# Moving the weights of the first unit and the order of the logits pairs in a fused encoder layer

## The chip, the cores and the metric

The kernel runs on one core of one Trainium2 chip. The metric is the device time of one execution in microseconds. The kernel before took 1164.75 us in the median of three runs (1164.25 to 1165.76). TensorE is called PE in the profile, VectorE DVE, ScalarE ACT, GpSimd POOL, SyncE SP.

## The reference

One layer of a streaming encoder over 640 tokens (512 of a prompt, 8 streams of 16 new frames), all in float32:

```python
def trunk_layer(x, pos, k_past, v_past, idxk_past, conv_prev, ...):
    x = x + 0.5 * swiglu(rmsnorm(x, ffn1_norm), ffn1_w_gate, ffn1_w_up, ffn1_w_down)
    h = rmsnorm(x, mix_norm)
    z = h @ w_in
    gb, gc, xv, q, k, v, qi, ki, wi = jnp.split(z, SPLIT_POINTS, axis=-1)
    conv_out = gb * conv                       # conv: 3 taps over gc * xv
    ...
    attn = dsa_attention(q, qi, wi, k_all, v_all, ki_all, pos, n_sel)
    x = x + jnp.concatenate([conv_out, attn], axis=-1) @ w_out
    x = x + 0.5 * swiglu(rmsnorm(x, ffn2_norm), ffn2_w_gate, ffn2_w_up, ffn2_w_down)
    return x, k, v, ki, conv_state
```

The width is 1024, the feed-forward parts have 2816 hidden columns. dsa_attention scores every key with a small indexer, keeps the best keys of each query (top_k), and does a masked softmax over them with 8 heads that share 2 key/value heads.

## The kernel before

Activations lie transposed, 128 of the 1024 columns to a chunk `c` (8 chunks), with 640 tokens along the free axis. A product of float32 accuracy is three products of rounded halves: of each operand there is a high half (`xh`, `wh`, written by ACT as a rounded copy) and a low half (`xl`, `wl`, which DVE writes as the difference), and PE multiplies high by high, low by high and high by low. Weights come in units of 128 x 2048 into `raw[:, slot]`, two slots in turn; a unit is split into halves (`split_hi`/`split_lo`, in quarters with `quarter_hi_of`/`quarter_lo_of`) once PE has used the unit two before it.

The program is: a feed-forward part `ffn(0)`, the projection of tokens with the indexer, the attention with the conv and output projections, and `ffn(1)`. Every engine has its own program, written out by hand in one order, and semaphores join them. Nothing is scheduled by a planner, but tables of numbers (`parts_by`, `issued_by`, `QUARTERS`, `ROUNDS`, `CONV_SPLITS`) say in which item a piece is put, on all engines at once.

**The first unit.** `first_unit` (L630 to L646) multiplies chunk by chunk as weights and activations arrive. Its weights are loaded in five pieces (`load_part`, L356), each with the chunk's gate columns and its up columns, 1024 columns apart in `raw`. Ahead of it PE does 16 float32 products of a tile of ones (`WARM_UP`, L988).

**A feed-forward part.** Four plain units come first. `plain_hid(3)` (L1647 and L1651) is what is left of the fourth: two DVE operations over 640 columns. It stands before the last pair of sets, `period(PAIRS - 1, ...)`. ACT's `rest_hi` later reads what it wrote.

**The attention.** There are 40 items, `ITEMS`: five token tiles in the order 3, 4, 2, 1, 0, of 8 heads or streams each. Tile 4 holds the streams' new frames (items 8 to 15, `logits_sample`, one to an item); the other tiles have `logits_pair` (L937), which puts the logits of items n and n+1 (n even) into banks 4 and 5. A pair needs both banks free, so it waits until DVE has read the logits of the two items before. What follows the logits of an item n:

- DVE: `masked_min(n)` (L2115; L2109 in tile 4) copies the masked logits out, finds their minimum and frees the bank;
- ACT: `exp_out(n)` (L1418; L1414 in tile 4);
- DVE, ACT or POOL: `normalise(n)`; from item 12 on it is POOL (L2353, L2354);
- PE: `turn_weights(n)` (L854) transposes the weights, ACT copies them out (`weights_out`), and PE multiplies them with the values: `weigh_sample_values(n)` (L965) in tile 4, else `weigh_four_heads(n)` (L979) in each fourth item.

In one pass of the loop over n, PE turns item n, issues the logits up to `issued_by(n)`, then does the parts up to `parts_by(n)` (`filler`: 6 matmuls of the conv or output projection, L596, L598, L600), then weighs. Items 12, 20, 28 and 36 have no part (`WITHOUT_PART`), and item 8 has none either, by `parts_by`. Four (after item 7) or eight (before) parts are a job, whose result DVE adds up in `proj_out`: L2077 for the output projection. On DVE the same loop has, in this order: `attended_lo` of a finished tile (L2134), `conv_lo`, `masked_min` of the items issued, top-8 rounds (`top_rounds`, L2062 and L2063, by the table `ROUNDS`) of the tiles still to come, `proj_out`, and the low half of a quarter of weights (`quarter_lo_of`, L1557).

Of the kernel before, what the change touches and what calls it, by code (L numbers as in the profile page):

```python
# [27 lines left out]
P = 128  # L28
# [44 lines left out]
def trunk(nc, xt, gu1, dn1, gu2, dn2, wtok, wconv, wout, small, gains, kcache, vcache, ikcache,  # L73
          conv_past, tables, bf_tables, x_keep, y_out, k_out, v_out, ik_out, conv_out):
    with ExitStack() as ctx:
# [154 lines left out]
        proj_job = sem("proj_job")  # L230
        proj_evac = sem("proj_evac")
# [69 lines left out]
        def parts_by(n):  # L301

            if n < 8:
                return 4 * (n + 1)
            return 32 + n - 8 - sum(m <= n for m in WITHOUT_PART)
# [11 lines left out]
        PROJ_SPLITS = {0: U_CONV + 5, item_of(9): U_OUT}  # L317
        QUARTERS = {14 + q: (U_OUT + 1, q) for q in range(4)}
# [4 lines left out]
        def issued_by(n):  # L323

            return min(n + 3 if n < 15 else 19 if n == 15 else n + 5, len(ITEMS))
# [4 lines left out]
        CONV_SPLITS = {8: (0,), 9: (1,), 10: (2,), 11: (3,)}  # L330
# [14 lines left out]
        def chunk_cols(flat, i):  # L345

            a, b = W_CHUNKS[i]
            return flat.rearrange("p (m n) -> p m n", m=2)[:, :, P * a:P * b]

        def quarters_before(U):  # L350
            return 3 * (0 if U == U_CONV else U - U_OUT)
# [232 lines left out]
        def _(pe):  # L584
# [41 lines left out]
            def first_unit():  # L626
# [3 lines left out]
                for c in range(C):  # L630
# [3 lines left out]
                    for m in range(2):  # L634
                        for o, t in zip(outs[m], cols):
                            pe.matmul(o, weight(wh, 0, 8 * m + c), xh[:, c, t], start=(c == 0), stop=False)
                    pe.wait_ge(*((part_lo, i + 1) if i < 4 else (lo_ready, 1)))
                    for m in range(2):
                        for o, t in zip(outs[m], cols):
                            pe.matmul(o, weight(wl, 0, 8 * m + c), xh[:, c, t], start=False, stop=False)  # L640
                    pe.wait_ge(xl_ready, c + 1)
                    for m in range(2):
                        for o, t in zip(outs[m], cols):
                            mm = pe.matmul(o, weight(wh, 0, 8 * m + c), xl[:, c, t], start=False,
# [245 lines left out]
            def proj_part(b, c):  # L890

                U = U_CONV + b // 2 if b < NPROJ else U_OUT + (b - NPROJ) // 4
                if c == 0:
                    pe.wait_ge(lo_ready, U + 1)
                    if U in (U_CONV, U_OUT + 1, U_OUT + 2):
# [204 lines left out]
        def _(act):  # L1100
# [34 lines left out]
            def ffn(k):  # L1135
# [212 lines left out]

                for n in (1, 2):
# [157 lines left out]
            for n in range(len(ITEMS)):  # L1507
                if n == 8 * (n // 8) in (8, 16):
                    attended_hi(n // 8 - 1)
                if n in CONV_SPLITS:  # L1510
                    act.wait_ge(proj_job, NPROJ)
# [10 lines left out]
                if n in QUARTERS and ITEMS[n][0] != 4:  # L1522
# [3 lines left out]
                if n in QUARTERS and ITEMS[n][0] == 4:  # L1526
# [9 lines left out]
        def _(dve):  # L1536
# [62 lines left out]
            def ffn(k):  # L1599
# [342 lines left out]
                plain_hid(3)  # L1942
# [301 lines left out]
            for n in range(len(ITEMS)):  # L2244
# [6 lines left out]
                for ahead in range(issued_by(n - 1), issued_by(n)):  # L2251
                    masked_min(ahead)
# [12 lines left out]
                if n in (25, 33):  # L2265
                    attended_lo(n // 8 - 1)
# [210 lines left out]
```

## Time and profile before

| | us |
|---|---|
| three runs | 1164.25, 1164.75, 1165.76 |
| the profiled execution | 1166.49 |
| its span, first to last instruction | 1164.6 |
| PE busy | 1154.6 |
| DVE busy | 916.1 |
| ACT busy | 526.1 |
| POOL busy | 94.7 |

The mean granted clock of TensorE is 0.994 of full speed. The profile comes from one execution. Busy shares are those of the whole span; a line's instructions are found by the line number. The numbers behind "idle before" in a timeline say how long an engine had stood still before the instruction, and what released it.

### The profile page before, as it was taken

Reading aid. Unit: us, or ns where it says so; the run is one execution under the profiler, and the core shown is the slowest. Engines: PE = TensorE matmul, PEld = TensorE weight load, DVE = VectorE, ACT = ScalarE, POOL = GpSimd, SP = SyncE. Lnnn points to the kernel's source line nnn. Section 1 sums busy time; section 2 is a strip of 40 time slices with the busy share of each in tenths; the row PEclk is TensorE's granted clock in tenths of the full one; section 3 lists DMA queues with packets and bytes.
Section 4 is the critical chain, followed back from the end, with each engine's and each line's share of the span. In section 5 each row is a group of like instructions: output and inputs, shape, how many; then the busy total and the mean of one; then the engine's idle time right before and its main releaser. Section 6 shows DMA issues by size and latency. Waiting matters only on the chain.

```text
span 1164.6 us, 20299 instructions
## 1 busy us (share of the span) xinstructions
PE 1154.6 (99%) x7704; PEld 1107.3 (95%) x7704; DVE 916.1 (79%) x1402; ACT 526.1 (45%) x791; POOL 94.7 (8%) x130
## 2 busy tenths in 40 slices
PE   9999999999999999999999899999999999999999
PEld 9999999999999999867987679999999999999998
DVE  6998777877989982467998753798877778798996
ACT  6354444444445552361234452434444444454452
POOL 0000000000000000102473351000000000000000
PEclk9999999999999999999999899999999999999999
DMA  7212221222332233201321023321322222124222
GB/s 249 85 55 91 86 95 72 98 82 67 124 146 80 73 109 119 73 37 37 145 73 37 1 67 107 129 73 37 109 72 84 96 72 98 64 100 154 103 87 84
DMA packets 22992, 103.98 MB, mean 89 GB/s; under 512 B 3344, under 2 KB 6288, under 8 KB 13584
## 3 DMA queue, kind: packets, MB, share of 16 engines
q1 hardware_dynamic: 21792, 99.67, 24.2%
q10 hardware_dynamic: 1136, 3.43, 1.0%
q8 instruction: 43, 0.70, 0.3%
q14 instruction: 21, 0.17, 0.0%
HBM read 96.99 MB, written 6.10 MB: 89 GB/s over the span
## 4 chain that ended last, share of the span: by engine, by line
PE 91%; DVE 7%; issue 1%; ACT 1%; DVEq 0%; POOL 0%; ACTq 0%; POOLq 0%
PE ps L656 18%; PE ps L658 18%; PE ps L657 18%; PE ps L596 8%; PE ps L600 8%; PE ps L598 8%; PE ps L587 2%; PE ps L589 2%; PE ps L588 2%; DVE score L2063 1%; PE ps L854 1%; DVE top L2062 1%; DVE wl L1548 1%; PE ps L937 1%; PE ps L863 1%
## 5 line engine op out<-in xcount | busy, mean ns | idle before, releaser
L1102 ACT ACTIVATE wh<-raw 128x1024 fp32r<-128x1024 f32 (+4 forms) x206 | 202.4, 985 | 261.6 <-PE ps L658 142.9
L656 PE MATMUL ps<-xs,wh 128*128 128x320 f32 x976 | 300.2, 308 | 0.5 <-ACT snap L1102 0.5
L657 PE MATMUL ps<-xs,wh 128*128 128x320 f32 x976 | 300.2, 308 | 0.0
L658 PE MATMUL ps<-xs,wl 128*128 128x320 f32 x976 | 300.1, 308 | 0.0
L656 PEld LDWEIGHTS ps<-xs,wh 128*128 128x128 f32 x976 | 182.9, 187 | 1.0 <-issue 1.0
L658 PEld LDWEIGHTS ps<-xs,wl 128*128 128x128 f32 x976 | 182.9, 187 | 0.0
L657 PEld LDWEIGHTS ps<-xs,wh 128*128 128x128 f32 x976 | 182.9, 187 | 0.0
L596 PE MATMUL ps<-xh,wh 128*128 128x320 f32 x544 | 131.1, 322 | 0.0
L1672 DVE TENSOR_TENSOR wl<-raw,wh 128x1024 fp32r<-128x1024 f32 (+1 forms) x108 | 112.7, 1044 | 19.4 <-ACT wh L1102 18.3
L600 PE MATMUL ps<-xh,wl 128*128 128x320 f32 x544 | 124.7, 311 | 0.0
L598 PE MATMUL ps<-xl,wh 128*128 128x320 f32 x544 | 124.6, 311 | 0.0
L1102 ACT ACTIVATE snap<-ps 128x320 f32<-128x320 f32 x156 | 68.0, 437 | 121.1 <-PE ps L658 120.6
L596 PEld LDWEIGHTS ps<-xh,wh 128*128 128x128 f32 x544 | 90.0, 189 | 12.6 <-issue 11.1
L598 PEld LDWEIGHTS ps<-xl,wh 128*128 128x128 f32 x544 | 91.8, 189 | 0.0
L600 PEld LDWEIGHTS ps<-xh,wl 128*128 128x128 f32 x544 | 91.7, 189 | 0.0
L658 PE MATMUL ps<-xr,wl 128*128 128x320 f32 x288 | 88.9, 309 | 0.0
L656 PE MATMUL ps<-xr,wh 128*128 128x320 f32 x288 | 88.9, 309 | 0.0
L657 PE MATMUL ps<-xr,wh 128*128 128x320 f32 x288 | 88.9, 309 | 0.0
L1672 DVE TENSOR_TENSOR wl<-sums,wh 128x1024 fp32r<-128x1024 f32 x36 | 44.1, 1225 | 38.1 <-ACT wh L1102 38.1
L1102 ACT ACTIVATE wh<-sums 128x1024 fp32r<-128x1024 f32 x52 | 54.8, 1053 | 24.0 <-DVE sums L1687 14.4
L1548 DVE TENSOR_TENSOR wl<-raw,wh 128x2048 fp32r<-128x2048 f32 (+2 forms) x31 | 56.5, 1823 | 11.5 <-ACT wh L1102 11.5
L1783 DVE TENSOR_TENSOR wl<-raw,wh 128x1024 fp32r<-128x1024 f32 (+1 forms) x48 | 49.9, 1041 | 6.1 <-ACT wh L1102 6.1
(282 smaller groups left out, 2134.4 us busy)
## 6 DMA issues: line engine op xcount, KB each, us to landing
raw<-gu SPq DMA_DIRECT2D x42, 1024.0 KB, 4.8
raw<-dn SPq DMA_DIRECT2D x16, 1024.0 KB, 5.3
raw<-dn SPq DMA_DIRECT2D x12, 512.0 KB, 3.8
raw<-wconv SPq DMA_DIRECT2D x6, 1024.0 KB, 4.9
raw<-wout SPq DMA_DIRECT2D x4, 1024.0 KB, 4.8
x<-xt SPq DMA_DIRECT2D x12, 320.0 KB, 4.7
raw<-wtok SPq DMA_DIRECT2D x4, 840.0 KB, 4.3
x_keep<-x SPq DMA_DIRECT2D x8, 320.0 KB, 2.2
```

The costliest lines, as they stand in the source:

```text
L587: pe.matmul(out, ah, bh, start=first, stop=False)
L588: pe.matmul(out, ah, bl, start=False, stop=False)
L596: pe.matmul(o, ah, bh[:, c], start=first, stop=False)
L598: pe.matmul(o, ah, bl[:, c], start=False, stop=False)
L600: last_mm = pe.matmul(o, al, bh[:, c], start=False, stop=last)
L656: pe.matmul(out, ah, bh, start=first, stop=False, skip_group_check=True)
L657: pe.matmul(out, ah, bl, start=False, stop=False, skip_group_check=True)
L658: return pe.matmul(out, al, bh, start=False, stop=last, skip_group_check=True)
L1102: return nc.scalar.activation(out, in_, ACT.Copy, scale=scale)
L1548: dve.tensor_tensor(wl[:, slot, 0:n], raw[:, slot, 0:n], wh[:, slot, 0:n].bitcast(F32), ALU.subtract).then_inc(lo_ready, 1)
L1672: dve.tensor_tensor(ring(wl_flat, part), set_source(slot, part), ring(wh_flat, part).bitcast(F32), ALU.subtract)\
L1783: dve.tensor_tensor(ring(wl_flat, part), set_source(slot, part), ring(wh_flat, part).bitcast(F32), ALU.subtract)\
```

## The change

Four things change.

1. The first unit of `ffn(0)` lies chunk by chunk in memory, and so in `raw`, `wh` and `wl`: the gate and up columns of one chunk side by side. PE reads weight tile 2c+m in place of 8m+c.
2. `plain_hid(3)` is issued by DVE inside the last period of a feed-forward part (the one with `ahead=False`), in place of before the last two; ACT waits for `hid_ready` before `rest_hi(1)`.
3. Item 8 gets a part, so that from there on each item does the part that was the next one's. With that go: `conv_hi`/`conv_lo` one item earlier (7 to 10), now released by a count of PE's part 27, `chunks_used`; and the weights of unit `U_OUT` split in quarters in items 4 to 7, in place of whole in item 3.
4. From item 15 on, PE issues logits behind the parts, and DVE does `masked_min` last in an item. `issued_by` is n+4 there and not n+5, so that pairs fall into odd items (15, 17, 19, ...) and not into even ones (15 for the first, then 16, 18, ...). ACT splits the quarter of item 15 before that item's `exp_out`.

```diff
@@ parts_by
-            return 32 + n - 8 - sum(m <= n for m in WITHOUT_PART)
+            return 32 + n - 7 - sum(m <= n for m in WITHOUT_PART)
...
-        PROJ_SPLITS = {0: U_CONV + 5, item_of(9): U_OUT}
-        QUARTERS = {14 + q: (U_OUT + 1, q) for q in range(4)}
+        PROJ_SPLITS = {0: U_CONV + 5}
+        QUARTERS = {4 + q: (U_OUT, q) for q in range(4)}
+        QUARTERS |= {14 + q: (U_OUT + 1, q) for q in range(4)}
...
-            return min(n + 3 if n < 15 else 19 if n == 15 else n + 5, len(ITEMS))
+            return min(n + 3 if n < 15 else n + 4, len(ITEMS))
...
-        CONV_SPLITS = {8: (0,), 9: (1,), 10: (2,), 11: (3,)}
+        CONV_SPLITS = {7: (0,), 8: (1,), 9: (2,), 10: (3,)}
@@ chunk_cols
-            return flat.rearrange("p (m n) -> p m n", m=2)[:, :, P * a:P * b]
+            return flat[:, 2 * P * a:2 * P * b]
@@ first_unit, three places
-                            pe.matmul(o, weight(wh, 0, 8 * m + c), xh[:, c, t], start=(c == 0), stop=False)
+                            pe.matmul(o, weight(wh, 0, 2 * c + m), xh[:, c, t], start=(c == 0), stop=False)
@@ proj_part
+                if b == NPROJ - 1 and c == 3:
+                    mm.then_inc(chunks_used, 1)
@@ PE, the loop over the items
-                for ahead in range(issued_by(n - 1), issued_by(n)):
-                    logits(ahead)
+                if n < 15:
+                    for ahead in range(issued_by(n - 1), issued_by(n)):
+                        logits(ahead)
                 for i in range(parts_by(n - 1), parts_by(n)):
                     filler(i)
+                if n >= 15:
+                    for ahead in range(issued_by(n - 1), issued_by(n)):
+                        logits(ahead)
@@ ACT, ffn and the items
+                act.wait_ge(hid_ready, PLAIN * (k + 1))
                 for n in (1, 2):
                     rest_hi(n)
...
-                    act.wait_ge(proj_job, NPROJ)
+                    act.wait_ge(chunks_used, 1)
...
-                if n in QUARTERS and ITEMS[n][0] != 4:
+                if n in QUARTERS and (ITEMS[n][0] != 4 or n == 15):
@@ DVE, period
+                    if not ahead:
+                        plain_hid(3)
                     out_of(p, slot, 0, block)
...
-                plain_hid(3)
                 period(PAIRS - 1, 0, pair_block(PAIRS - 1))
@@ DVE, the items
-                for ahead in range(issued_by(n - 1), issued_by(n)):
-                    masked_min(ahead)
+                if n < 15:
+                    for ahead in range(issued_by(n - 1), issued_by(n)):
+                        masked_min(ahead)
...
+                if n >= 15:
+                    for ahead in range(issued_by(n - 1), issued_by(n)):
+                        masked_min(ahead)
@@ the layout on the host, gate_up
+        if first_by_chunk:
+            plain[0] = plain[0].reshape(P, 2, C, P).transpose(0, 2, 1, 3).reshape(P, 2 * C * P)
```

What it does to the order of PE in item 15. Before, from the turn of item 15 on (`tab` holds the identity, L854 is the turn, L937 the pair, L596 to L600 a part, L965 the weighing):

```order
L854 MATMUL ps<-tab,score 128x128 [waits bank6_free,p_sample_ready]
L854 MATMUL ps<-tab,score 128x128 x2
L937 MATMUL ps<-kt,q_all 128x384 [waits bank5_free,bank4_free]
L937 MATMUL ps<-kt,q_all 128x384
L596 MATMUL ps<-xh,wh 128x320 x2
L598 MATMUL ps<-xl,wh 128x320 x2
L600 MATMUL ps<-xh,wl 128x320 x2
L965 MATMUL ps<-hid,ikc_v 64x64 [waits bank6_free]
L965 MATMUL ps<-hid,ikc_v 64x64
L965 MATMUL ps<-hid,zkv 64x64
L965 MATMUL ps<-hid,ikc_v 64x64 x2
L965 MATMUL ps<-hid,zkv 64x64
```

After, from the same turn on (L856 is the turn, L598 to L602 a part, L941 the pair):

```order
L856 MATMUL ps<-tab,score 128x128 [waits bank6_free,p_sample_ready]
L856 MATMUL ps<-tab,score 128x128 x2
L598 MATMUL ps<-xh,wh 128x320 x2
L600 MATMUL ps<-xl,wh 128x320 x2
L602 MATMUL ps<-xh,wl 128x320 x2
L941 MATMUL ps<-kt,q_all 128x384 [waits bank5_free,bank4_free]
L941 MATMUL ps<-kt,q_all 128x384
L969 MATMUL ps<-hid,ikc_v 64x64 [waits bank6_free]
L969 MATMUL ps<-hid,ikc_v 64x64
L969 MATMUL ps<-hid,zkv 64x64
L969 MATMUL ps<-hid,ikc_v 64x64 x2
L969 MATMUL ps<-hid,zkv 64x64
```

The part, which stood behind the pair (18, 19), now stands ahead of it; the pair comes last before the weighing. The next pair, (20, 21), stood behind the turn of item 16 and now stands behind the part of item 17.

What it does to the order of DVE from `masked_min(16)` in item 14 on. Before (L2115 is `masked_min`, L2062 and L2063 a top-8 round, L1557 a quarter):

```order
L2115 ISA rp,stat<-ps,mask 128x384 [waits bank6_full,mask_ready,bank4_full]
L2115 ISA stat 128x1
L2062 MAX top8<-score 128x8
L2063 MATCH_REPLACE score<-top8,score 128x256 [waits vector_chain]
L1557 TENSOR_TENSOR wl<-raw,wh 128x512 [waits quarter_hi,vector_chain]
L2115 ISA rp,stat<-ps,mask 128x384 [waits bank6_full,mask_ready,bank5_full]
L2115 ISA stat 128x1
L2115 ISA hid,stat<-ps,mask 128x384 [waits bank6_full,mask_ready,bank4_full]
L2115 ISA stat 128x1
L2062 MAX top8<-score 128x8
L2063 MATCH_REPLACE score<-top8,score 128x256 [waits vector_chain]
```

After (L2125, L2072 and L2073, L1566):

```order
L2125 ISA rp,stat<-ps,mask 128x384 [waits mask_ready,bank6_full,bank4_full,vector_chain]
L2125 ISA stat 128x1
L2072 MAX top8<-score 128x8
L2073 MATCH_REPLACE score<-top8,score 128x256 [waits vector_chain]
L1566 TENSOR_TENSOR wl<-raw,wh 128x512 [waits quarter_hi,vector_chain]
L2072 MAX top8<-score 128x8
L2073 MATCH_REPLACE score<-top8,score 128x256 [waits vector_chain]
L1566 TENSOR_TENSOR wl<-raw,wh 128x512 [waits quarter_hi,vector_chain]
L2125 ISA rp,stat<-ps,mask 128x384 [waits bank6_full,mask_ready,bank5_full]
L2125 ISA stat 128x1
L2125 ISA hid,stat<-ps,mask 128x384 [waits bank6_full,mask_ready,bank4_full]
L2125 ISA stat 128x1
```

`masked_min(17)`, which frees bank 5 for the pair (18, 19), stood behind the round and the quarter of item 14. It has moved behind those of item 15 as well. The `attended_lo` of item 16 (L2134, then L2144) keeps its place between `masked_min(18)` and `masked_min(19)`.

## Rows read from the trace of the kernel before

**Rows 1.** The page, part 1: engine, busy us, share of the span, instructions.

```profile
PE 1154.6 (99%) x7704; PEld 1107.3 (95%) x7704; DVE 916.1 (79%) x1402; ACT 526.1 (45%) x791; POOL 94.7 (8%) x130
```

**Rows 2.** Waits of PE, whole span: reader, releaser, us in total, times, longest.

```profile
PE ps L937 <- DVE stat L2115: 4.0, 3, 2.4
...
PE ps L656 <- ACT snap L1102: 0.5, 2, 0.2
```

**Rows 3.** Stretches of 2 us: length, busy us by engine, PEclk, DMA.

```profile
658.00:660.00 2.00, 0.09 (x2) 0.12 (x2) 1.25 (x4) 1.07 (x3) 1.59 (x2) 0.81 0.00 0
...
672.00:674.00 2.00, 2.00 (x11) 1.08 (x10) 1.89 (x4) 0.86 (x3) 1.45 (x2) 0.78 0.00 0
```

**Rows 4.** Timeline of PE: start, length, instruction, idle before it.

```profile
637.96 0.47 PE L965 MATMUL ps<-hid,ikc_v 128*64 128x64 f32 x6 [0.35 <-ACT hid L1102]
...
638.93 0.55 PE L854 MATMUL ps<-tab,rp 128*128 128x128 f32 x3 [0.26 <-DVE rp L2127]
...
640.37 0.56 PE L596 MATMUL ps<-xh,wh 128*128 128x320 f32 x2
...
641.45 0.50 PE L965 MATMUL ps<-hid,ikc_v 128*64 128x64 f32 x6
...
656.97 0.55 PE L854 MATMUL ps<-tab,score 128*128 128x128 f32 x3
659.91 1.65 PE L937 MATMUL ps<-kt,q_all 64*128 64x384 f32 x4 [2.39 <-DVE stat L2115]
...
663.38 0.75 PE L965 MATMUL ps<-hid,ikc_v 128*64 128x64 f32 x6
...
664.49 0.90 PE L854 MATMUL ps<-tab,rp 128*128 128x128 f32 x3
666.53 1.65 PE L937 MATMUL ps<-kt,q_all 64*128 64x384 f32 x4 [1.14 <-DVE stat L2115]
668.12 0.90 PE L596 MATMUL ps<-xh,wh 128*128 128x320 f32 x2
...
669.88 0.84 PE L854 MATMUL ps<-tab,rp 128*128 128x128 f32 x3
```

**Rows 5.** Timeline of DVE in the same place.

```profile
650.26 0.56 DVE L2109 TENSOR_REDUCE stat<-ps 128x1 f32<-128x384 f32 x1 [0.56 <-PE ps L926]
...
655.93 0.82 DVE L2077 SCALAR_TENSOR_TENSOR x<-ps,x 128x640 f32<-128x640 f32 x1
656.67 0.55 DVE L2115 CUSTOM_DVE_ANT_0 rp<-ps,mask 128x384 f32<-128x384 f32 x1
...
657.14 0.42 DVE L2062 MAX8 top<-score 128x8 f32<-128x256 f32 x1
...
658.59 0.69 DVE L1557 TENSOR_TENSOR wl<-raw,wh 128x512 fp32r<-128x512 f32 x1 [0.51 <-ACT wh L1102]
659.20 0.55 DVE L2115 CUSTOM_DVE_ANT_0 rp<-ps,mask 128x384 f32<-128x384 f32 x1
...
661.56 0.56 DVE L2115 CUSTOM_DVE_ANT_0 hid<-ps,mask 128x384 f32<-128x384 f32 x1 [1.80 <-PE ps L937]
...
665.23 0.69 DVE L2134 TENSOR_TENSOR xl<-ps,xh 128x512 fp32r<-128x512 f32 x1 [1.04 <-ACT xh L1102]
```

**Rows 6.** Timeline of POOL: the scaling of one item's weights.

```profile
661.23 0.59 POOL L2354 TENSOR_SCALAR rp<-rp,stat 128x384 f32<-128x384 f32 x1
```

**Rows 7.** Timeline of DVE in the first feed-forward part.

```profile
266.85 0.83 DVE L1651 TENSOR_TENSOR hid<-hid,glu_u 128x640 f32<-128x640 f32 x1
...
279.93 0.49 DVE L1706 TENSOR_TENSOR quart<-ps,snap 128x320 f32<-128x320 f32 x1 [0.87 <-PE ps L658]
```

**Rows 8.** Timeline of all engines at the start.

```profile
1.18 6.74 PE L988 MATMUL ps<-ones 128*128 128x128 f32 x32 [1.18 <-POOL cstate L2302]
...
6.83 0.42 DVE L1606 TENSOR_TENSOR wl<-raw,wh 128x256 fp32r<-128x256 f32 x1 [6.83 <-ACT wh L1102]
...
7.68 0.82 PE L636 MATMUL ps<-xh,wh 128*128 128x320 f32 x4
```

More of the change, by code:

```diff
@@ L230, in trunk @@
         proj_job = sem("proj_job")
+        chunks_used = sem("chunks_used")
         proj_evac = sem("proj_evac")
@@ L347, in chunk_cols @@
             a, b = W_CHUNKS[i]
-            return flat.rearrange("p (m n) -> p m n", m=2)[:, :, P * a:P * b]
+            return flat[:, 2 * P * a:2 * P * b]
         def quarters_before(U):
-            return 3 * (0 if U == U_CONV else U - U_OUT)
+            return 3 * (0 if U == U_CONV else 1 + U - U_OUT)
         def first_part(buf, i):
@@ L639, in first_unit @@
                         for o, t in zip(outs[m], cols):
-                            pe.matmul(o, weight(wl, 0, 8 * m + c), xh[:, c, t], start=False, stop=False)
+                            pe.matmul(o, weight(wl, 0, 2 * c + m), xh[:, c, t], start=False, stop=False)
                     pe.wait_ge(xl_ready, c + 1)
@@ L643, in first_unit @@
                         for o, t in zip(outs[m], cols):
-                            mm = pe.matmul(o, weight(wh, 0, 8 * m + c), xl[:, c, t], start=False,
+                            mm = pe.matmul(o, weight(wh, 0, 2 * c + m), xl[:, c, t], start=False,
                                            stop=(c == C - 1))
@@ L894, in proj_part @@
                     pe.wait_ge(lo_ready, U + 1)
-                    if U in (U_CONV, U_OUT + 1, U_OUT + 2):
+                    if U in (U_CONV, U_OUT, U_OUT + 1, U_OUT + 2):
                         pe.wait_ge(quarter_lo, quarters_before(U) + 3)
@@ L1525, in _ @@
                     exp_out(ahead)
-                if n in QUARTERS and ITEMS[n][0] == 4:
+                if n in QUARTERS and ITEMS[n][0] == 4 and n != 15:
                     quarter_hi_of(*QUARTERS[n])
@@ L2399, in lay_out, with gate_up @@
     x_all = np.concatenate([a["x_prompt"].reshape(SEQ, D), a["x_sample"].reshape(NB * NT, D)])
-    def gate_up(g, u):
+    def gate_up(g, u, first_by_chunk):
         both = np.stack([g[0], u[0]]).reshape(2, C, P, NF, P)
         plain = both[:, :, :, :PLAIN].transpose(3, 2, 0, 1, 4).reshape(PLAIN, P, 2 * C * P)
+        if first_by_chunk:
+            plain[0] = plain[0].reshape(P, 2, C, P).transpose(0, 2, 1, 3).reshape(P, 2 * C * P)
         sets = both[:, :, :, PLAIN:].reshape(2, C, P, PAIRS, 2, P)
@@ L2430, in lay_out @@
         "xt": x_all.reshape(TOK, C, P).transpose(2, 1, 0),
-        "gu1": gate_up(a["ffn1_w_gate"], a["ffn1_w_up"]), "dn1": down(a["ffn1_w_down"]),
-        "gu2": gate_up(a["ffn2_w_gate"], a["ffn2_w_up"]), "dn2": down(a["ffn2_w_down"]),
+        "gu1": gate_up(a["ffn1_w_gate"], a["ffn1_w_up"], True), "dn1": down(a["ffn1_w_down"]),
+        "gu2": gate_up(a["ffn2_w_gate"], a["ffn2_w_up"], False), "dn2": down(a["ffn2_w_down"]),
         "wtok": np.stack([filled(cols(tok[h * 512:(h + 1) * 512, s:s + n]))
```

## The prediction

> **What bounds the kernel now.** I read the page first: PE is busy for 1154.6 of 1164.6 us [rows 1], so no more than 10 us can come from waits, unless matmuls themselves run slow somewhere. Then the waits of PE: most of what the trace explains is one line, the logits pair, which waits 4.0 us in three places for DVE's `masked_min`; a set of a feed-forward part waits 0.5 us in two places [rows 2]. Then the stretches of 2 us: the granted clock is full everywhere but for one place. In 658 to 660 it is 0.81, so 0.76 us of these 2 us ran at half speed (0.19 / 0.5 x 2) and the clock fell at 659.24; in 672 to 674 it is 0.78, so it rose at 672.88 [rows 3]. For 13.64 us PE ran at 1.2 GHz and not at 2.4 GHz. The timeline of PE shows what went ahead: the pair (18, 19) of item 15 waits 2.39 us for `masked_min(17)`, and the clock falls 1.72 us into this wait; the pair (20, 21) waits 1.14 us, and the clock rises 6.35 us after that wait ends [rows 4]. Of the 13.64 us, PE stood still for 0.67 us (659.24 to 659.91) and for 1.14 us. The other 11.83 us would have taken half as long, so the low clock costs 5.9 us: more than all waits of the place together. The change works in this place.
>
> **The start.** The first unit's chunks now come as one run per partition and not as two. PE's warm-up takes from 1.18 to about 7.7 us; the low half that the first unit needs is begun by DVE at 6.83 and takes 0.42 us, and the first real matmul runs at 7.68 [rows 8]. The data is there 0.4 us before PE is. A load that comes sooner is hidden by the warm-up, and copies and matmuls keep their shapes: 0. Were the warm-up no cover, it would be worth 0.4 us at most.
>
> **The move of `plain_hid(3)`.** Its two operations stand before the next-to-last period, and 266.85 is the second of them [rows 7]; the work behind it comes late, and PE waits for a snapshot. That wait occurs once in each feed-forward part, 0.5 us in all [rows 2]. In the last period DVE has nothing to prepare for a next set; it stood still for 0.87 us before its first output, at 279.93 [rows 7]. Two operations of 0.83 us there push this output by about 0.8 us, and the wait for PE's next products behind it absorbs that. Saved 0.5 us (bounds: 0 if the wait moves along, 0.5). ACT's new wait costs nothing: what stands ahead of it waits for the end of the last set, and that set needs an output which DVE gives behind `plain_hid(3)`. Queued behind the wait are `rest_hi` 1 and 2.
>
> **A part in item 8.** A part and what surrounds it take 1.08 us (640.37 to 641.45 [rows 4]). PE's two small waits, 0.35 us in item 8 and 0.26 us in item 9 [rows 4], go, since ACT's copy and DVE's scaling keep their time while PE comes later. So every item from 9 to 15 starts 1.08 - 0.61 = 0.47 us later with one part more done: 0.61 us saved. The splits moved with it (conv, quarters of `U_OUT`) fall in items where each engine keeps up; a quarter is 0.69 us of DVE and replaces, four for one, a split of the whole unit. I take 0, with 0.5 us lost as the other bound.
>
> **The pair (18, 19).** From `masked_min(14)` at 650.26 on, DVE has no gap except for one of 0.51 us for ACT, until `masked_min(17)` at 659.20 [rows 5]: DVE itself sets the wait. That is 8.94 us. Out of it goes `proj_out(12)` (655.93 to 656.67: 0.74), which now belongs to item 11. Into it come a top-8 round (0.94: it starts at 657.14 and its three instructions fill DVE until 658.08) and the quarter of item 15 (0.61, 658.59 to 659.20). So 9.75 us. `masked_min(14)` comes with PE's item 12, at 650.73, `masked_min(17)` at 660.48, and the pair 0.71 us behind it as before: 661.19. PE is done with turn 15 at 657.52 + 0.47 and with the part, half of 1.76 us (668.12 to 669.88 at the low clock [rows 4]), at 658.87. The wait is 2.32 us. It stays: what the part fills, the later `masked_min` opens again. Saved 0.07 us.
>
> **The clock.** With a wait of the same length, work ahead of it of about the same kind, I take it that the clock falls as before, 1.72 us into the wait, at 660.6, and rises 6.35 us after the last long wait. If that is now this one, it rises at 667.5. Then 6.35 us of work run at the low clock and cost 3.2 us, where it was 5.9: 2.7 us saved. This is the largest term, and it hangs on the second wait.
>
> **The pair (20, 21).** It now stands in item 17 behind the part. At the low clock PE needs from 661.19: the pair 1.65, the weighing 1.11, turn 0.90, part 1.76, turn 0.84 [rows 4]: 667.45, then a part at full clock 0.88: 668.33. DVE: `masked_min(18)` 1.65 behind the pair; `attended_lo` 1.85 us behind the start of the weighing (663.38 to 665.23 [rows 4, 5]), at 664.69, 0.61 long; a round, 666.24; `proj_out(13)` only when PE's part of item 16 is done (661.19 + 1.65 + 1.11 + 0.90 + 1.76 = 666.61), until 667.44; a quarter, 668.05; `masked_min(19)` and the 0.71 us: 668.76. So this wait is 0.43 in place of 1.14 us: 0.71 saved. Behind it, by the same durations, the pair (22, 23) waits some 0.2 us for `masked_min(21)`, which is new.
>
> **The sum.** 0.5 + 0.61 + 0.07 + 2.7 + 0.71 - 0.2 = 4.4 us. The profiled execution took 1166.49 us and becomes 1162.1; it lies 1.74 us above the median, so against the median of 1164.75 the forecast is 1160.4 us.
>
> On the price of the clock the Trainium skill (TensorE: Matmul & The Clock Gate, Terms) counts the throttled time times (1 - K/N), idle or not. By that the stretch of before costs half of 13.64, 6.8 us, and that of after half of 6.9, 3.5 us: the gain would be 3.4 and the forecast 1159.7 us. The trace shows PE idle in 1.8 us of it, which no clock can shorten [rows 3, 4], and the sum stays with that.
>
> **Rivals.**
> - The clock never falls. For it: one more part of dense matmuls lies just before the wait. Against it: the wait has its old length. PE then comes to the pair (20, 21) at about 665.2, but DVE, bound by the exponential of item 18 and its own queue, frees bank 5 only for 667.5. The gain is 1.3 us more than forecast, 5.7 us: 1159.1 us.
> - The clock survives the first wait and falls in the second, which is then 2.3 us long. 5.7 - 3.2 = 2.5 us gained: 1162.3 us.
> - The low clock lasts as long as before, since a pair, a weighing and a turn follow the wait again, and between 659.91 and 665.39 such work did not raise it. Then 5.9 us are lost as before, and 4.4 - 2.7 = 1.7 us are gained: 1163.1 us.
> - Slower: pairs come too late for their turns. From the start of `masked_min` to the end of POOL's scaling pass 2.62 us (659.20 to 661.82 [rows 5, 6]), 4.0 with the pair and the first of two ahead of it, and the odd item's `masked_min` stands behind one more round. PE has turns 18 and 19, two parts, a pair and the weighing between, some 4.9 us at full clock. If ACT and POOL are a microsecond late, each item waits, and the clock stays down to about item 24 (685): 24 us of low clock cost 12.0, not 3.2 us, and 4.4 becomes -4.4: 1169.2 us. It turns slower once low-clock work exceeds 6.35 + 2 x 4.4 = 15 us. Against it: at the low clock PE leaves more room, not less.
>
> **Chances.** Forecast 0.50, never falls 0.08, falls in the second wait 0.14, as long as before 0.18, slower 0.10. A measurement of this kernel tells 0.2%, 2.3 us, from no change. The forecast (its own range 1159.2 to 1162), the first rival and most of the second are faster by more than that, and a little of the third: 0.72. The rest of these two is within it: 0.18. The slower case has 0.10. The range from 1158.6 to 1164.6 us leaves out that case and a little at the lower end.
>
> **What would show it.** PE's waits: none at items 8 and 9, none for the snapshot at about 271 us, one of about 2.3 us for the pair (18, 19), one below 0.6 for (20, 21). The granted clock: one stretch below full speed, about 7 us long. The start: the first real matmul at 7.7 us as before. Wrong would be a first wait below 1.5 us, a stretch at the low clock over 10 us, or waits of turns for POOL behind item 18.

## The result

| | us (median) | lowest to highest | executions |
|---|---|---|---|
| before | 1164.75 | 1163.61 to 1166.27 | 9 |
| after | 1168.45 | 1168.05 to 1170.66 | 9 |

The ratio is 1.0033 [1.0024, 1.0043]: the changed kernel is slower, by 3.7 us. The forecast was 1160.4 us. The nine executions of after have mean granted clocks of 0.996 (the 1170.66 us), 0.999 (five of them) and 1.000 (three).

The profiled execution of after took 1168.05 us (span 1166.1). The page, part 1, answers to [rows 1], and the clock of the core follows it:

```profile
PE 1148.8 (99%) x7704; PEld 1102.4 (95%) x7704; DVE 918.6 (79%) x1405; ACT 525.7 (45%) x794; POOL 95.1 (8%) x130
```

```profile
core 0: 1166.1 us, clock 1.000
```

PE is busy 5.8 us less with the same 7704 matmuls: in this execution the clock never fell between the first matmul and the last. All the same the span is 1.5 us longer, so PE stands still 7.3 us more. The waits of PE over the whole span (reader, releaser, us in total, times, longest) answer to [rows 2]:

```profile
PE ps L941 <- DVE stat L2125: 6.9, 5, 2.3
PE ps L856 <- ACT hid L1110: 3.2, 5, 1.7
...
PE ps L983 <- ACT hid L1110: 0.9, 2, 0.5
PE ps L856 <- DVE rp L2137: 0.8, 1, 0.8
```

Pairs (L941) wait for DVE in five places, and turns (L856) wait for ACT's copy `weights_out` in five: 3.2 us in one line, where the page of before has 0.2. The snapshot waits (L656 before) are gone. The timeline of PE shows where; it answers to [rows 4]:

```profile
661.26 0.92 PE L941 MATMUL ps<-kt,q_all 64*128 64x384 f32 x4 [2.31 <-DVE stat L2125]
664.49 0.52 PE L856 MATMUL ps<-tab,rp 128*128 128x128 f32 x3 [0.30 <-ACT hid L1110]
667.63 0.92 PE L941 MATMUL ps<-kt,q_all 64*128 64x384 f32 x4 [1.74 <-DVE stat L2125]
668.75 0.52 PE L856 MATMUL ps<-tab,hid 128*128 128x128 f32 x3 [0.20 <-ACT hid L1110]
671.82 0.52 PE L856 MATMUL ps<-tab,score 128*128 128x128 f32 x3 [1.67 <-ACT hid L1110]
676.66 0.52 PE L856 MATMUL ps<-tab,rp 128*128 128x128 f32 x3 [0.67 <-ACT hid L1110]
...
690.46 0.70 PE L941 MATMUL ps<-kt,q_all 64*128 64x256 f32 x4 [1.15 <-DVE stat L2125]
...
695.41 0.49 PE L941 MATMUL ps<-kt,q_all 64*128 64x128 f32 x4 [1.28 <-DVE stat L2125]
```

The pair (18, 19) waits 2.31 us and comes at 661.26, as forecast (2.32, 661.19). It takes 0.92 us and not 1.65: the wait did not lower the clock. Behind it, up to 720 us, before has two waits, 1.14 us at the pair (20, 21) and 0.18 us; after has eleven, of 0.18 to 1.74 us and 8.4 us in all. Seven of them stand in these lines. Why turn 19 waits (671.82) is read from DVE and ACT together:

```profile
667.52 0.61 ACT L1427 ACTIVATE score<-score,stat 128x384 f32<-128x384 f32 x1 [2.65 <-DVE stat L2125]
...
668.50 0.62 ACT L1110 ACTIVATE wh<-raw 128x512 fp32r<-128x512 f32 x1
669.23 0.85 DVE L1566 TENSOR_TENSOR wl<-raw,wh 128x512 fp32r<-128x512 f32 x1 [0.88 <-ACT wh L1110]
670.00 0.54 DVE L2125 CUSTOM_DVE_ANT_0 rp<-ps,mask 128x384 f32<-128x384 f32 x1
...
670.59 0.62 ACT L1427 ACTIVATE rp<-rp,stat 128x384 f32<-128x384 f32 x1 [1.47 <-DVE stat L2125]
...
671.20 0.47 ACT L1110 ACTIVATE hid<-ps 128x384 f32<-128x384 f32 x1
```

DVE's low half of a quarter (669.23) waits for ACT's high half (668.50). `masked_min(20)` (670.00) stands behind that quarter, `exp_out(20)` (670.59) waits for `masked_min(20)`, and ACT's `weights_out(18)` (671.20) stands behind `exp_out(20)`. Turn 19 needs it. So the two queues hand one task to and fro. For turn 19 this is not the whole cause: with `masked_min` in front it waits as long, 1.65 us (see the experiments). Items 26 to 28 show the exchange undiluted:

```profile
687.67 0.41 DVE L2125 CUSTOM_DVE_ANT_0 hid<-ps,mask 128x256 f32<-128x256 f32 x1
...
688.12 0.51 ACT L1427 ACTIVATE hid<-hid,stat 128x256 f32<-128x256 f32 x1 [1.59 <-DVE stat L2125]
...
688.63 0.61 ACT L1110 ACTIVATE wh<-raw 128x512 fp32r<-128x512 f32 x1
...
689.28 0.69 DVE L1566 TENSOR_TENSOR wl<-raw,wh 128x512 fp32r<-128x512 f32 x1 [1.19 <-ACT wh L1110]
689.89 0.42 DVE L2125 CUSTOM_DVE_ANT_0 hid<-ps,mask 128x256 f32<-128x256 f32 x1
...
690.35 0.51 ACT L1427 ACTIVATE hid<-hid,stat 128x256 f32<-128x256 f32 x1 [1.10 <-DVE stat L2125]
```

From one `masked_min` to the next is 2.22 us (687.67 to 689.89), with both engines standing still for more than a microsecond of it. Before, `masked_min` stood ahead of the quarter, and ACT's exponential ran beside DVE's low half:

```profile
691.86 0.62 ACT L1102 ACTIVATE wh<-raw 128x512 fp32r<-128x512 f32 x1
...
692.66 0.29 DVE L2115 CUSTOM_DVE_ANT_0 rp<-ps,mask 128x128 f32<-128x128 f32 x1 [0.47 <-PE ps L937]
692.88 0.84 DVE L1557 TENSOR_TENSOR wl<-raw,wh 128x512 fp32r<-128x512 f32 x1
693.00 0.40 ACT L1418 ACTIVATE rp<-rp,stat 128x128 f32<-128x128 f32 x1 [0.52 <-DVE stat L2115]
```

At the start PE's first real matmul runs at 6.52 us (7.68 in [rows 8]), but the column sums behind the first unit wait:

```profile
1.18 5.58 PE L992 MATMUL ps<-ones 128*128 128x128 f32 x32 [1.18 <-POOL cstate L2316]
6.52 0.82 PE L638 MATMUL ps<-xh,wh 128*128 128x320 f32 x4
...
24.14 1.28 PE L609 MATMUL ps<-ones,sq_pair 128*128 128x1 f32 x10 [0.62 <-DVE sq_pair L1580]
```

The warm-up's own length varies from execution to execution (5.30 to 6.74 us in the profiles of this study), which moves the first matmul about as much: it ran at 6.25 us in one profile of the old layout.

### The profile page after: what moved, and what is told of

Its sections match the earlier page's. It is cut to its first block, busy times and chain, and to the rows that moved or that the text cites. A ratio compares the mean times of both kernels' runs of the same rounds, so it can differ in the third digit from the quotient of the medians.

```text
span 1166.1 us, 20306 instructions
## 1 busy us (share of the span) xinstructions
PE 1148.8 (99%) x7704; PEld 1102.4 (95%) x7704; DVE 918.6 (79%) x1405; ACT 525.7 (45%) x794; POOL 95.1 (8%) x130
## 4 chain that ended last, share of the span: by engine, by line
PE 86%; DVE 9%; issue 2%; ACT 1%; DMA 1%; SPq 0%; POOL 0%; DVEq 0%; ACTq 0%
PE ps L658 18%; PE ps L659 18%; PE ps L660 18%; PE ps L598 7%; PE ps L602 7%; PE ps L600 7%; PE ps L589 2%; PE ps L591 2%; PE ps L590 2%; DVE score L2073 2%; DVE top L2072 2%; DVE wl L1557 1%; PE ps L865 1%; PE ps L856 1%; DMA x<-xt 1%
## 5 line engine op out<-in xcount | busy, mean ns | idle before, releaser
L598 PE MATMUL ps<-xh,wh 128*128 128x320 f32 x544 | 130.0, 320 | 0.2 <-issue 0.2
L602 PE MATMUL ps<-xh,wl 128*128 128x320 f32 x544 | 123.9, 309 | 0.0
L600 PE MATMUL ps<-xl,wh 128*128 128x320 f32 x544 | 123.9, 309 | 0.0
L598 PEld LDWEIGHTS ps<-xh,wh 128*128 128x128 f32 x544 | 89.3, 188 | 10.3 <-issue 8.9
L602 PEld LDWEIGHTS ps<-xh,wl 128*128 128x128 f32 x544 | 91.0, 188 | 0.0
L600 PEld LDWEIGHTS ps<-xl,wh 128*128 128x128 f32 x544 | 90.8, 188 | 0.0
L1557 DVE TENSOR_TENSOR wl<-raw,wh 128x2048 fp32r<-128x2048 f32 (+2 forms) x30 | 54.2, 1807 | 11.5 <-ACT wh L1110 11.5
```

The lines of the kernel that those rows point to most:

```text
L598: pe.matmul(o, ah, bh[:, c], start=first, stop=False)
L600: pe.matmul(o, ah, bl[:, c], start=False, stop=False)
L602: last_mm = pe.matmul(o, al, bh[:, c], start=False, stop=last)
L1557: dve.tensor_tensor(wl[:, slot, 0:n], raw[:, slot, 0:n], wh[:, slot, 0:n].bitcast(F32), ALU.subtract).then_inc(lo_ready, 1)
```

## The experiments

Every kernel ran beside the kernel before on one chip; the ratio is to that, with its 95% interval. The last column is the mean granted clock of the executions. Where two experiments are compared below by their medians, they may come from different chips and sets, whose medians of before differ by up to 0.6 us; the ratios give the same differences within 0.6 us.

| kernel | us (median) | ratio | clock |
|---|---|---|---|
| before (medians of the five sets) | 1164.15 to 1164.75 | | 0.994 to 1.000 |
| before, run as a kernel of its own | 1163.99 | 0.9998 [0.9988, 1.0007] | 0.994 to 0.998 |
| parts 1 to 3 | 1161.93 | 0.9981 [0.9971, 0.9990] | 0.997 to 1.000 |
| part 4 alone | 1169.32 | 1.0038 [1.0024, 1.0052] | 0.997, 0.999 |
| after, `masked_min` in front | 1161.57 | 0.9974 [0.9963, 0.9985] | 0.999, 1.000 |
| ... and pairs ahead of the parts | 1162.41 | 0.9986 [0.9976, 0.9995] | 0.999, 1.000 |
| ... and exponentials later | 1161.20 | 0.9973 [0.9962, 0.9985] | 1.000 |
| after, `masked_min` ahead of the quarter | 1163.54 | 0.9995 [0.9985, 1.0004] | 0.998 to 1.000 |
| part 1 alone | 1163.80 | 0.9998 [0.9989, 1.0007] | 0.998 to 1.000 |
| part 2 alone | 1163.56 | 0.9995 [0.9986, 1.0004] | 0.994 to 0.999 |
| part 3 alone | 1163.98 | 0.9994 [0.9985, 1.0003] | 0.996 to 0.999 |
| exponentials later, rounds later | 1158.81 | 0.9954 [0.9940, 0.9967] | 1.000 |
| before, waits filled | 1162.62 | 0.9983 [0.9974, 0.9992] | 1.000 |

**The kernel before again.** No edit.

> The kernel before, unchanged, to read the granted clock of several executions beside their times. Theory A (the low clock is a fixed part of this kernel, 13.6 us of it in each execution): every execution shows a mean clock of 0.994 and they differ only by noise. Theory B (the low clock depends on how the wait falls in time, and the profiled execution had more of it than most): mean clocks spread from about 0.994 to 0.998, and times follow them, up to 3 us apart. Both: ratio 1.000.

1163.99 us, with mean clocks from 0.994 (1166.11 us) to 0.998: Theory B. The stretches of 2 us of the profiled execution (1163.03 us, clock 0.998) against [rows 3]:

```profile
658.00:660.00 2.00, 0.28 (x2) 0.31 (x4) 1.17 (x3) 1.07 (x3) 1.45 (x2) 1.00 0.00 0
660.00:662.00 2.00, 2.00 (x19) 1.27 (x17) 1.33 (x5) 1.08 (x5) 1.14 (x2) 1.00 0.00 0
...
664.00:666.00 2.00, 1.52 (x7) 1.00 (x8) 0.94 (x5) 0.71 (x2) 0.74 (x2) 0.89 0.00 0
666.00:668.00 2.00, 2.00 (x10) 1.96 (x9) 1.55 (x5) 0.90 (x3) 1.50 (x3) 0.50 0.00 0
668.00:670.00 2.00, 2.00 (x13) 1.63 (x11) 1.93 (x6) 1.79 (x5) 0.54 (x2) 0.76 0.00 0
```

The first wait (657.34 to 659.72) is as long as in the profile of before, 2.38 us, and the clock stays at 2.4 GHz through it; it is down only behind the second wait, for 0.44 + 2.00 + 0.96 = 3.4 us (each stretch's loss over 0.5, times 2). The 13.64 us of the prediction were one execution's, at the low end of what this kernel does.

**Without the order of part 4.** The changed kernel with part 4 undone on all engines.

> The changed kernel with the order of logits, masked minima and the issue table put back (parts 1 to 3 of the change alone). Theory A (the whole loss is in the order): 0.5 us for the snapshot waits and 0.6 us for items 8 and 9 are gained on the kernel before, 1163.6 us. Theory B (the part in item 8, the quarters or the first unit cost something too): not faster than before, 1165 us or more.

1161.93 us: parts 1 to 3 gain 2.4 us, more than Theory A has, and there are no turn waits for ACT beyond 0.2 us. The slowdown is part 4's: 1168.45 - 1161.93 = 6.5 us.

**Part 4 alone.** The kernel before with the new order and `issued_by`.

> The kernel before with the new order alone (part 4 of the change). Theory A: the loss of the changed kernel plus the 1.1 us that its other parts gain, 1169.5 us. Theory B: the order alone costs less, 1166 us or below, since part of the loss comes from the other parts.

1169.32 us, as Theory A has it: 5 us slower than the median beside it, 4.4 us by the ratio. Most of the waits of after behind item 18 are there (turns 1.48 and 0.67 us, a pair 1.28); its first pair waits 3.10 us.

**`masked_min` in front.** The changed kernel, one edit of DVE's order:

```diff
-                if n < 15:
-                    for ahead in range(issued_by(n - 1), issued_by(n)):
-                        masked_min(ahead)
+                for ahead in range(issued_by(n - 1), issued_by(n)):
+                    masked_min(ahead)
...
-                if n >= 15:
-                    for ahead in range(issued_by(n - 1), issued_by(n)):
-                        masked_min(ahead)
```

> The changed kernel, PE and ACT untouched, DVE's masked minimum back in front of the top-8 rounds and the quarter of its item. Theory A (DVE's place for the masked minimum makes the loss: it frees the banks late, and from item 26 on DVE and ACT hand each other quarter, minimum and exponential one after another, 2.2 us an item): most of the 10.7 us of waits behind item 15 go; with the clock up, 1160 to 1163 us. Theory B (PE's pairs behind the parts and in odd items leave too little time before their turns): waits of the turns for ACT and POOL stay, 1167 us or more.

1161.57 us, 6.9 us less than after, in the range of Theory A. The waits of PE in its profile:

```profile
PE ps L856 <- ACT hid L1110: 2.9, 4, 1.6
...
PE ps L941 <- DVE stat L2125: 1.2, 2, 0.7
```

The waits of pairs fall from 6.9 to 1.2 us. Those of turns for ACT hardly fall, from 3.2 to 2.9, and turn 19 still waits 1.65 us; one turn waits 0.5 us for POOL. With pairs in even items and ahead of the parts (parts 1 to 3 alone) turns wait 0.2 us for ACT. So these waits come with PE's new order, as Theory B said, and not with DVE's.

**`masked_min` ahead of the quarter only.** It goes behind the rounds and `proj_out`, but ahead of `quarter_lo_of`.

> The changed kernel (1168.45 us) with DVE's masked_min from item 15 on ahead of the quarter of the weights, still behind the top-8 rounds and proj_out. With masked_min ahead of all three it took 1161.57 us: 6.9 us less. Theory A: most of it is the quarter, which waits for ACT's quarter_hi while ACT waits for masked_min (items 15 to 17 and 26 to 28): 1163.5 us (1162.5 to 1165), no wait of a pair or a turn above 0.6 us in items 26 to 29, and 1 to 1.7 us left at items 15 to 19, where rounds and proj_out stand ahead. Theory B: it is the rounds and proj_out, 0.94 and 0.74 us each in items 15 to 19: 1167 us.

1163.54 us. So the place behind the quarter is worth 1168.45 - 1163.54 = 4.9 us (4.4 by the ratios), that behind the rounds and `proj_out` 1163.54 - 1161.57 = 2.0 (2.4). The waits of pairs in items 26 to 29 are gone; a turn there waits 0.45 us for POOL. In items 15 to 19 more is left than Theory A has: pairs wait 1.70 and 0.26 us, turns 0.20 and 0.66. The 4.9 us hold two things that no run parts: the quarter's own 0.6 us of DVE in front of a `masked_min`, as ahead of the pair (18, 19), where the quarter of item 15 waited for nothing (2.31 against 1.70 us of PE's wait); and the exchange with ACT.

**Pairs ahead of the parts.** `masked_min` in front, and PE's order of before, still in odd items.

> The kernel with masked_min in front (1161.57 us), and PE's logits pairs again ahead of the parts, still in odd items. There the wait of the pair (18, 19) was 0.72 us and the turn of item 19 waited 1.65 us for ACT's copy. Theory A: a pair's place within its item is worth little. The pair (18, 19) comes a part (0.88 us) earlier to the same masked_min(17) and waits 1.6 us; the pair (20, 21) and with it masked_min(20) and exp_out(20) come a part earlier to ACT, so turn 19 waits 0.8 us: the sum stays, 1161.6 us (1161.0 to 1162.5). Theory B: it is the place behind the part that makes the pair late for ACT, and its undoing gains most of the 2.6 us of turn waits: 1159.5 us.

1162.41 us, in the range of Theory A. The pair (18, 19) waits 1.59 us, turn 19 1.00 us, and three more pairs 0.29, 0.43 and 0.62. A pair behind the part gains 0.8 us by the medians, 1.4 by the ratios, whose intervals overlap: most of the waits shift.

**The exponentials later.** `masked_min` in front, and in ACT's loop:

```diff
-                for ahead in range(issued_by(n - 1), issued_by(n)):
+                first, last = (n - 1, n) if n < 17 else (n - 2, n) if n % 2 == 0 else (n, n)
+                for ahead in range(issued_by(first), issued_by(last)):
                     exp_out(ahead)
```

> The kernel with masked_min in front (1161.57 us), and from item 18 on ACT issues the exponentials of both items of a pair in the even item behind weights_out, where the first of the two stood in the odd item ahead of the next weights_out. Theory A: PE's turns 19, 21 and 23 wait 1.65, 0.67 and 0.26 us because weights_out stands in ACT's queue behind an exponential that waits for a masked_min. Then these waits all but go (below 0.5 us together) and the time is 1159.5 us (1159.0 to 1160.3). Theory B: the exponentials then come too late for POOL's scaling and the waits move to the turns of items 20 and 22, for POOL, or to the next pair for DVE: 1161.5 us, no change.

1161.20 us. Turn 19's wait of 1.65 us is gone, but the next pair waits in its place:

```profile
669.46 0.92 PE L941 MATMUL ps<-kt,q_all 64*128 64x384 f32 x4 [1.38 <-DVE stat L2126]
```

What is late there is DVE's own queue, which has no gap from 660.94 to 670.2 us: `masked_min`, rounds, `attended_lo`, `proj_out` and quarters. Theory B holds.

**Rounds later.** The last kernel, and on DVE:

```diff
-                  1: {n: 1 for n in (0, 1, 3, 5, 6, 7, 8, 9, 12, 13, 14, 15, 16, 17, 18, 19)}}
+                  1: {n: 1 for n in (0, 1, 3, 5, 6, 7, 8, 9, 12, 13, 15, 18, 19)} | {20: 3}}
...
-                for i in CONV_SPLITS.get(n, ()):
-                    conv_lo(i)
                 if 8 <= n + 1 < GPSIMD_FROM:
                     normalise(n + 1)
+                for i in CONV_SPLITS.get(n, ()):
+                    conv_lo(i)
```

> The kernel with the exponentials later (1161.2 us), and two edits of DVE's order: the top-8 rounds of tile 1 in items 14, 16 and 17 move to item 20, where DVE stands still for 2 to 3.7 us between two masked_min; and normalise(n+1) stands ahead of conv_lo in items 8 to 10. Theory A: DVE's own queue sets what PE waits for in items 15 to 18 (0.72 and 1.38 us of pairs, 0.67 of a turn), and conv_lo the 0.81 us of turn 9. Then the wait of turn 9 falls below 0.2 us, those of the pairs below 0.4 us together, and the time is 1158.8 us (1158.0 to 1159.8). Theory B: PE's pair itself sets masked_min, and the chain from there by exp_out to the turn is what is late; the rounds then hide beside it, only turn 9 gains, and the three rounds in item 20 make the pair behind it late: 1160.6 us or more.

1158.81 us, 5.3 us faster than the kernel before beside it and 9.6 us faster than after, on the forecast of Theory A. Turn 9 no longer waits. The pairs still wait more than it has, 0.65 us in this one place against 0.4 in all. The first waits of PE behind item 14:

```profile
658.43 0.92 PE L941 MATMUL ps<-kt,q_all 64*128 64x384 f32 x4 [0.65 <-DVE stat L2126]
661.67 0.52 PE L856 MATMUL ps<-tab,rp 128*128 128x128 f32 x3 [0.30 <-ACT hid L1110]
665.56 0.55 PE L856 MATMUL ps<-tab,score 128*128 128x128 f32 x3 [0.30 <-POOL score L2365]
670.43 0.52 PE L856 MATMUL ps<-tab,rp 128*128 128x128 f32 x3 [0.67 <-ACT hid L1110]
```

**Parts 1, 2 and 3, one at a time.**

> The kernel before with part 1 alone: the first unit's weights chunk by chunk. Theory A, that of the prediction: the start is covered by PE's warm-up, and the time stays, 1164.3 us (ratio 1.000, 0.9993 to 1.0007), with the first unit's column sums at 24.5 us and no wait of PE there. Theory B: PE starts some 0.4 us earlier and keeps it: 1163.9 us, and the attention begins 0.4 us earlier. The profile tells these apart better than the time.

> The kernel before with part 2 alone: plain_hid(3) inside the last period. Theory A: the two snapshot waits of 0.25 us go and nothing else changes: 1163.8 us (0.5 less; ratio 0.9996). Theory B: parts 1 to 3 gained 2.4 us where the prediction has 1.1, and the rest lies here, because the stretch behind the last period also gets shorter: 1163.0 us or less.

> The kernel before with part 3 alone: a part in item 8, with its splits one item earlier and unit U_OUT in quarters. The prediction had 0.6 us saved at items 8 and 9 and 0.07 us at the pair (18, 19). With parts 1 and 2 as well, turn 9 waited 0.8 us for DVE's scaling, where it had waited 0.26 us, and the pairs (18, 19) and (20, 21) waited 1.6 us each. Theory A: a part placed in item 8 shortens the wait of the pair (18, 19) from 2.4 to 1.6 us, since PE comes to it 0.5 us later and masked_min(17) keeps its own time or comes earlier: 1163.1 us (1.2 less). Theory B: 0.6 us less, 1163.7 us, and the rest of the 2.4 us lies in parts 1 and 2.

By their ratios 0.2, 0.6 and 0.7 us, 1.5 in all; each interval is 1 us to both sides, so no one of them is told from nothing. Part 1: in its profile the first real matmul runs at 6.82 us (7.43 and 7.68 in the two profiles of before), and a wait of 0.62 us for the column sums takes most of that back. Over all profiles the column sums come at 24.01 to 25.16 us with the old layout (six, mean 24.66) and at 24.14 to 24.82 with the new one (eight, mean 24.44): what the layout is worth stays open between 0 and 0.4 us. With the old layout PE waits 0.20 to 0.52 us for ACT's `wh` at the first chunks in three of the six profiles, with the new one 0.16 us in one of the eight: the warm-up does not cover the first chunks in every execution. Part 2: the snapshot waits are gone. Part 3: turn 9 waits 0.81 us in place of 0.26, the pair (18, 19) 1.59 in place of 2.38, as Theory A has it.

**The waits filled.** The kernel before; PE multiplies ones in its waits for bank 5:

```diff
                 for k in (n, n + 1):
                     wait_bank_free(pe, ("logit", k))
+                    for _ in range({18: 9, 20: 5}.get(k, 0)):
+                        pe.matmul(ps[:, bank(("logit", n)), 0:P], ones[:, :], ones[:, :], start=True, stop=True)
```

> The kernel before, with PE doing 9 products of the tile of ones while it waits for bank 5 ahead of the pair (18, 19), and 5 ahead of the pair (20, 21), in bank 4, which is free and is overwritten by the pair. Nothing else changes. At full clock a product takes some 0.2 us, so that they fit into waits of 2.4 and 1.1 to 1.6 us. It tells what the low clock costs: the executions of the kernel before have mean granted clocks of 0.994 to 1.000. Theory A: while PE runs at half speed DVE goes on, and PE finds its next bank free sooner, so most of the loss is taken back at the next wait; by the line through the executions of the kernel before, 0.48 us for each 0.001 of mean clock, a full clock gives 0.5 to 0.9 us against the median: 1163.5 us, with a spread below 1 us and none above 1164.5 us. Theory B, the price of the prediction: half of PE's busy time at the low clock, 1.8 us for a mean clock of 0.998: 1162.3 us. Theory C: the clock falls all the same, and nothing changes: 1164.2 us with executions up to 1166.

1162.62 us, 1162.21 to 1162.91, every execution at clock 1.000. That is 2.1 us less than the median beside it (2.0 by the ratio [0.9 to 3.0]), nearer to Theory B, and 3.9 us less than the profiled execution of [rows 1]. The median beside it is the highest of these sets: against the median of 98 executions of the kernel before (88 beside the experiments and the ten of the kernel before again), 1164.3 us, it is 1.7 us. The four of these at clock 1.000 have a mean of 1163.0 us, 1.3 us under that median. But the two profiles also show what Theory A said. PE at the pair (20, 21), at the next pair and at the first turn of a later item, without the filling (1163.03 us, clock 0.998):

```profile
664.48 0.92 PE L937 MATMUL ps<-kt,q_all 64*128 64x384 f32 x4 [1.64 <-DVE stat L2115]
...
669.51 0.92 PE L937 MATMUL ps<-kt,q_all 64*128 64x384 f32 x4
...
672.64 1.51 PE L979 MATMUL ps<-hid,zkv 128*64 128x256 f32 x12
...
676.88 0.52 PE L854 MATMUL ps<-tab,hid 128*128 128x128 f32 x3 [0.18 <-ACT hid L1102]
```

With it:

```profile
663.97 0.92 PE L939 MATMUL ps<-kt,q_all 64*128 64x384 f32 x4 [0.45 <-DVE stat L2117]
...
667.70 0.92 PE L939 MATMUL ps<-kt,q_all 64*128 64x384 f32 x4 [0.20 <-DVE stat L2117]
...
671.89 1.52 PE L981 MATMUL ps<-hid,zkv 128*64 128x256 f32 x12 [0.98 <-ACT hid L1104]
...
676.14 0.52 PE L854 MATMUL ps<-tab,hid 128*128 128x128 f32 x3 [0.18 <-ACT hid L1104]
```

From the first pair to the second it takes 5.03 us with the low clock (for 3.4 us of them) and 3.73 at the full one: 1.3 us. Of these the faster kernel gives back 0.98 us in a wait for ACT ahead of a weighing (L981) that the slower one (L979) does not have; from the first pair to the turn the difference is 12.40 - 12.17 = 0.2 us.

## Why the prediction was wrong

**The step that failed is the end of "The pair (20, 21)": "Behind it, by the same durations, the pair (22, 23) waits some 0.2 us for `masked_min(21)`, which is new."** That term stands for all that the new order costs in the items to 39. It was 0.2 us. The pair (22, 23) did not wait at all; the place of `masked_min` alone is worth 6.9 us (1168.45 against 1161.57). With it, part 4 lost 6.5 us (1168.45 against 1161.93) where its terms gain 3.3 (0.07 + 2.7 + 0.71 - 0.2). I followed DVE's queue up to item 17 with durations only, and took ACT as an engine that answers at once. I did not lay the new DVE order beside ACT's order, where `quarter_hi_of` stands ahead of `exp_out`: in items 26 to 28 each of the two queues waits for the other once per item, ten items behind the place that I looked at. 4.9 of the 6.9 us come from the place behind the quarter, at items 15 to 17 and 26 to 28, and 2.0 from that behind rounds and `proj_out`. How much of the 4.9 is the exchange and how much the quarter's own time stays open.

**The first wait** was right to 0.1 us (2.32 forecast, 2.31 found), and so was the time of the pair. The second was forecast at 0.43 us and took 1.74. The working had the clock low until 667.45 and PE ready for the pair at 668.33; with the clock up PE was ready at 665.89, 2.4 us earlier. DVE was early too, by 1.1 us: `masked_min(19)` at 666.93 in place of 668.05. The difference, 1.3 us, is the longer wait. (One sum of that paragraph is off by its own rows: `proj_out(13)` from 666.61 with 0.74 us ends at 667.35 and not 667.44, so the forecast wait was 0.34 us. That changes nothing here.)

**The clock** was the largest term, and wrong in three ways. It did not fall in the profiled execution of the changed kernel, although the wait ahead of it had the same length, and in the other eight it fell little or not at all (mean clock 0.999 or 1.000) but for one at 0.996. Its price was read from one execution at a mean clock of 0.994, while most executions of the kernel before have 0.998 or 0.999. As busy time the price was right (5.9 us forecast, PE 5.8 us less busy), but it is not what the kernel gains: with the waits filled, 3.9 us less than the profiled execution, and 2.1 us less than the median beside it. And the sum took the 1.74 us by which that execution lay above the median off again at its end, though these were mostly the clock's: over 98 executions of the kernel before, the mean time is 1166.4 us at clock 0.994 and 1163.9 to 1164.0 at 0.998 and 0.999. The gain was counted twice. The Trainium skill (TensorE: Matmul & The Clock Gate, Terms) puts the penalty at the total time at the low clock times (1 - K/N). By that the estimate for the profiled execution is 6.8 us, further still from the 3.9 that the filled waits gave.

**Item 8** was forecast as two small waits gone, 0.61 us. The one at item 8 went; that at turn 9 grew from 0.26 to 0.81 us. The splits moved with the part were put at nothing. Yet `conv_lo(1)`, which now stands in item 8 ahead of DVE's `normalise(9)`, took 0.7 us longer than `conv_lo(0)` did in its place. It overlaps POOL's last operation of a convolution for 0.9 us, where the one before overlapped it for 0.2 us. Before, then after:

```profile
636.11 1.55 POOL L2339 TENSOR_TENSOR conv_o<-conv_o,sq_pair 128x640 f32<-128x640 f32 x1
637.47 0.88 DVE L2099 TENSOR_TENSOR xl<-conv_o,xh 128x640 fp32r<-128x640 f32 x1
```

```profile
636.34 1.87 POOL L2353 TENSOR_TENSOR conv_o<-conv_o,sq_pair 128x640 f32<-128x640 f32 x1 [1.71 <-DVE sq_pair L2104]
637.31 1.59 DVE L2109 TENSOR_TENSOR xl<-conv_o,xh 128x640 fp32r<-128x640 f32 x1
```

With `normalise` ahead of `conv_lo` (rounds later) the wait of turn 9 was gone. The pair (18, 19) waited 1.59 us in place of 2.38 with part 3 and DVE's old order, which is more than the two small waits together.

**`plain_hid(3)`** was right: the waits of 0.25 us are gone from both feed-forward parts, 0.5 us. **The start** at 0 is not contradicted. Parts 1 to 3 together gained 2.4 us (by the ratio 2.2 [1.2 to 3.4]) where the terms had 1.1 to 1.2; one at a time they sum to 1.5 us. The runs do not settle which of them gave more than its term.

**The rivals.** "The clock never falls" came true for the place that it works out: it has the pair (20, 21) freed at 667.5 with PE there at 665.2, and the pair came at 667.63 with PE there at 665.89. Its time, 1159.1 us, was wrong by the same missing term as the forecast's. The slower rival had nearly the right time (1169.2 us) for a wrong reason, which is luck: turns did come late, yet for ACT's copies and not for POOL's scaling, and the clock had no part in it. It was given 0.10, and its price was argued by the low clock alone.

The account of the 3.7 us, by medians: from before to parts 1 to 3, -2.4; pairs behind the parts and in odd items, with `masked_min` kept in front, -0.4, which is not told from nothing; `masked_min` behind rounds and `proj_out`, +2.0; behind the quarter too, +4.9. Together +4.1, from 1164.34 us beside the first kernels; from the 1164.75 us beside after it is 3.7.

## What to carry to other kernels

When a step moves in one in-order queue, write that queue beside each queue it exchanges with, for every item that the loop covers, and look for the pattern "A waits for B, B's next waits for A's next": it turns two engines that could work side by side into a series (2.22 us from one `masked_min` to the next in items 26 to 28), and a sum of durations along one engine does not show it. A wait that such a chain explains can have a second cause behind it: turn 19 waited as long once the chain was gone. A step that frees a bank and starts a chain belongs ahead of work that only has a far due time, and slack is found by looking for the gaps of the same engine (rounds moved from items 14, 16 and 17 to item 20: with one more swap, 2.4 us). Before a term is read from one profile, see whether the profiled execution lies off the median, and do not subtract its surplus a second time.

## What the runs showed of the hardware

- The same program has different clocks. In the kernel before, a wait of 2.38 or 2.39 us let the clock fall 1.72 us into it in one execution and not at all in another; over 98 executions the mean clock is 0.994 in 9 of them, 0.998 or 0.999 in 60 and 1.000 in 4. In the changed kernel a wait of 2.31 us did not lower it.
- The clock can fall behind a wait and not in it. With `masked_min` ahead of the quarter, a wait of 1.70 us ended at 660.97, PE was busy from there on, and the clock was at half speed from about 662:

```profile
660.00:662.00 2.00, 1.03 (x8) 0.51 (x9) 0.90 (x4) 0.71 (x2) 0.35 (x1) 0.99 0.00 0
662.00:664.00 2.00, 2.00 (x17) 1.88 (x17) 1.34 (x4) 1.42 (x4) 1.84 (x3) 0.50 0.00 0
```

- With fourteen products of ones in two waits the mean clock was 1.000 (2.4 GHz) in all 11 executions, and the spread of the times fell from 3.7 us (1162.67 to 1166.40, 15 executions beside it) to 0.7 us.
- Operations of DVE and POOL that overlap do not both keep their own speed. `conv_lo` (DVE, 128x640) takes 0.81 to 0.88 us in all places but two. In item 8, in the seven profiles with part 3 and `conv_lo` ahead of `normalise`, it takes 1.58 or 1.59 us (0.81 with `normalise` ahead) and in the changed kernel it overlaps an operation of POOL there for 0.9 us; in item 7 it takes 2.19 us and overlaps one for 1.5 us. At 647.28 us of the kernel before it keeps its 0.83 us, and POOL's scaling beside it takes 1.27 us in place of 0.59. That the overlap is the cause is read from these rows; no run changed the overlap alone.
- The sixteen products of ones ahead of the first matmul took 5.30 to 6.74 us in the fourteen profiles.
